# The opening of a two-block transformer kernel: modulation columns and first projection in one program

## What is computed

```python
mod = jax.nn.silu(c) @ w_ada[l] + b_ada[l]          # c: 1 x 1024, w_ada: 1024 x 6144
sh1, sc1, g1, sh2, sc2, g2 = jnp.split(mod[:, None, :], 6, axis=-1)
h = modulate(rmsnorm(x, norm_mix_g[l]), sh1, sc1)    # h * (1 + sc1) + sh1
x = x + g1 * hybrid_mixer(h, w_in[l], ...)           # proj = h @ w_in is its first product
```

## Time and profile before

| | us |
|---|---|
| median of 3 runs | 1884.81 |
| lowest, highest run | 1880.37, 1891.37 |
| profiled execution, its own time | 1885.66 |
| span of the profiled execution | 1883.9 |
| start of the first projection matmul in the span | 48.15 |
| PE busy in the span | 1730.2 |

### The profile page before, as it was taken

One profiled execution on the slowest core, in us unless ns is written; L12 is line 12 of the kernel. 1 busy time (PEld: TensorE's weight loads), 2 busy tenths in 40 slices (PEclk: granted clock), 3 DMA queues, 4 the chain that ended last, 5 costly groups with the idle time before them and its releaser, 6 DMA issues. The chain is left out here.

```text
span 1883.9 us, 20211 instructions
## 1 busy us (share of the span) xinstructions
PE 1730.2 (92%) x8167; PEld 1182.2 (63%) x8167; DVE 805.9 (43%) x1275; ACT 529.4 (28%) x891; POOL 49.2 (3%) x89
## 2 busy tenths in 40 slices
PE   2999989879979999999989999999899989899878
PEld 2887866636668888878768876757334434344346
DVE  4763357632462322255632275234423323233255
ACT  4212246731242222232533242324100000000045
POOL 0000000100000000000000000000200000000000
PEclk8999989999989999999989999999999999999989
DMA  9664120022422222231312011218799999999951
GB/s 354 215 260 139 44 107 28 2 90 90 146 78 90 89 90 90 90 109 59 134 67 101 34 46 45 90 58 347 261 426 426 425 427 427 425 428 426 427 234 45
DMA packets 87655, 351.75 MB, mean 187 GB/s; under 512 B 9910, under 2 KB 39266, under 8 KB 71561
## 3 DMA queue, kind: packets, MB, share of 16 engines
q1 hardware_dynamic: 85002, 346.08, 46.8%
q0 software_dynamic: 2560, 4.37, 0.7%
HBM read 346.03 MB, written 8.43 MB: 188 GB/s over the span
## 5 line engine op out<-in xcount | busy, mean ns | idle before, releaser
L547 DVE TENSOR_TENSOR arena<-ring,arena 128x1024 fp32r<-128x1024 f32 x120 | 146.9, 1225 | 242.9 <-ACT arena L596 223.8
L2651 PE MATMUL ex_h<-ring,u_big_tail 128*64 128x512 f32 x512 | 152.3, 603 | 12.9 <-DMA ring<-in_w 7.8
L552 PE MATMUL up_ps<-h_high,arena 128*128 128x512 f32 x352 | 139.3, 396 | 6.7 <-PEq L178 6.2
L553 PE MATMUL up_ps<-arena 128*128 128x512 f32 x352 | 139.8, 397 | 0.0
L554 PE MATMUL up_ps<-h_high,arena 128*128 128x512 f32 x352 | 139.7, 397 | 0.0
L596 ACT CAST arena<-ring 128x1024 fp32r<-128x1024 f32 x82 | 85.8, 1046 | 167.3 <-PE up_ps L554 88.8
L2651 PE MATMUL ex_h<-s_ab,u_big_tail 128*64 128x512 f32 x272 | 114.3, 596 | 2.3 <-DVE u_big_tail L2622 1.4
L2622 DVE TENSOR_TENSOR u_big_tail<-ex_x,vcol 128x512 f32<-128x512 f32 x32 | 20.6, 687 | 179.7 <-PE ex_x L2615 169.7
L2651 PEld LDWEIGHTS ex_h<-ring,u_big_tail 128*64 128x64 f32 x512 | 47.1, 138 | 76.7 <-issue 75.7
L2917 ACT ACTIVATE u_big_tail<-ex_h 128x512 f32<-128x512 f32 x16 | 9.6, 597 | 292.5 <-PE ex_h L2651 292.5
L552 PEld LDWEIGHTS up_ps<-h_high,arena 128*128 128x128 f32 x352 | 66.5, 189 | 23.4 <-issue 6.6
(11 more groups left out here) (578 smaller groups left out, 3593.8 us busy)
## 6 DMA issues: line engine op xcount, KB each, us to landing
ring<-in_w SPq DMA_DIRECT2D x42, 2048.0 KB, 32.6
s_ab<-in_w SPq DMA_DIRECT2D x32, 2048.0 KB, 31.9
ring<-in_w_in SPq DMA_DIRECT2D x19, 2048.0 KB, 8.0
ring<-in_w_ada SPq DMA_DIRECT2D x24, 1024.0 KB, 6.8
reg_a<-in_w SPq DMA_DIRECT2D x10, 2048.0 KB, 31.9
w1flat<-in_w SPq DMA_DIRECT2D x10, 2048.0 KB
ring<-in_w_ffn_gate SPq DMA_DIRECT2D x11, 1024.0 KB, 5.3
ring<-in_w_ffn_up SPq DMA_DIRECT2D x11, 1024.0 KB, 7.8
```

The lines of the kernel that those rows point to most:

```text
L547: return engine.tensor_tensor(lo, v, hi.bitcast(F32), ALU.subtract)
L552: nc.tensor.matmul(ps, x[0], y[0], start=start, stop=False)
L553: nc.tensor.matmul(ps, x[0], y[1], start=False, stop=False)
L2651: mm = nc.tensor.matmul(ps[half, :], xT[:, k, half], ws[j][:, k, cols], start=(k == 0), stop=(k == k_end - 1))
```

## The change

`stage_modulation` keeps only the name of the row buffer. Its work moves into a class `Opening`, whose methods are called at the head of each engine's list in `stage_project1`; the barrier between the two is gone. In it

- SP loads `c` directly into a column block of `vcol`, 8 neighbouring values for each partition, ahead of `x`; the nine small vectors and `g_ffn_2` (also directly as columns) come between slabs 1 and 2; and 128 columns of `w_in` (`w_first`, 0.5 MB) come ahead of slab 7, as the first unit of the projection.
- DVE adds slabs 0 to 4 only (`ON_DVE = 5`). PE sums `acc` against ones, and slabs 5, 6 and 7 each with their own column of silu(c) as the moving operand, straight from `ring`. The 16 columns are split into two groups with a PSUM bank each, `g` 0 and 1, for feature tiles 0 to 3 and 4 to 7.
- PE's transposes no longer wait for a slab. ACT copies them to a place of their own (`raws`), takes epsilon and 1/D into its root, and loads that table ahead of `x`.
- ACT writes the high part of `h` directly from `raws` with scale and bias (L449 of the new file), and for tiles 1, 3 and 5 (`ON_ACT`) also the full value (L452); DVE makes the full value of the other five (L420) and all low parts. The casts L582 of eight tiles are gone.
- POOL clears `acc2` after the sums are done and after the first unit has been used.

The core of the diff; lines of plumbing are left out:

```diff
+    def sync(self, sp):
+        b, a = self.b, self.b.a
+        sp.dma_start(b.vcol[:, NV + KD:NV + 2 * KD], a["c"].rearrange("a (p k) -> (a p) k", p=P)).then_inc(self.c_in, 16)
+        sp.dma_start(b.x[:], a["x"][0].rearrange("(t p) d -> p t d", p=P)).then_inc(self.x_in, 16)
+        for k in range(KD):
+            if k == 2:
+                for name, n in VROWS:
...
+            if k == KD - 1:
+                sp.dma_start(self.w_first, feature_tiles(a["w_in"][0], 0, P)).then_inc(self.w_in, 16)
+            sp.dma_start(self.piece(k), b.ada1[:, k, :]).then_inc(self.landed[k], 16)
...
+    def tensor(self, pe):
...
+        pe.wait_ge(self.cols_out, 1)
+        for g in range(2):
+            nc.tensor.matmul(psc[g][:, 0:2 * KD], b.ident[:], bias, start=True, stop=False, skip_group_check=True)
+
+        def column_sums(slab, by, g, stop=False):
+            for i in range(2):
+                for k in range(4 * g, 4 * g + 4):
+                    n = i * KD + k
+                    mm = nc.tensor.matmul(psc[g][:, n:n + 1], slab[:, n * P:n * P + P], by, start=False,
+                                          stop=stop and i == 1 and k == 4 * g + 3, skip_group_check=True)
+            return mm
+        pe.wait_ge(self.slabs, ON_DVE)
+        for g in range(2):
+            column_sums(self.acc, b.ones[:, 0:1], g)
+        for k in range(ON_DVE, KD):
+            pe.wait_ge(self.landed[k], 16)
+            for g in range(2):
+                mm = column_sums(self.piece(k), b.sc[:, k:k + 1], g, k == KD - 1)
+                if k == KD - 1:
+                    mm.then_inc(self.summed, 1)
+            if k % 2 and k < KD - 1:
+                mm.then_inc(b.ring_used[k // 2], 1)
...
+            for k in range(4 * g, 4 * g + 4):
+                if k in ON_ACT:
+                    dve.wait_ge(self.made_a, ON_ACT.index(k) + 1)
                 else:
-                    dve.wait_ge(added, k)
...
+                    dve.wait_ge(self.raw, k + 1)
+                    nc.vector.tensor_scalar(b.hT[:, k, :], self.raws[k], b.mulcol[:, k:k + 1], b.modcol[:, k:k + 1],
+                                            ALU.mult, ALU.add).then_inc(self.made, 1)
+                    dve.wait_ge(self.made, k + 1 - sum(j < k for j in ON_ACT))
+                dve.wait_ge(parts.h_hi, k + 1)
+                lower(nc.vector, parts.h[1][:, k, :], b.hT[:, k, :], parts.h[0][:, k, :]).then_inc(parts.h_lo, 1)
...
+        parts.act_w(act, 0)
+        for k in range(KD):
+            act.wait_ge(self.raw, k + 1)
+            act.wait_ge(self.mul, k // 4 + 1)
+            nc.scalar.activation(parts.h[0][:, k, :], self.raws[k], ACT.Identity, scale=b.mulcol[:, k:k + 1],
+                                 bias=b.modcol[:, k:k + 1]).then_inc(parts.h_hi, 1)
+            if k in ON_ACT:
+                nc.scalar.activation(b.hT[:, k, :], self.raws[k], ACT.Identity, scale=b.mulcol[:, k:k + 1],
+                                     bias=b.modcol[:, k:k + 1]).then_inc(self.made_a, 1)
...
         @block.gpsimd
         def _(pool):
+            op.pool(pool)
+            pool.wait_ge(op.summed, 2)
+            pool.wait_ge(parts.used, 1)
             nc.gpsimd.memset(b.acc2, 0.0).then_inc(cleared, 1)
```

More of the change, by code:

```diff
@@ L267 @@
          ("g_ple_2", 8), ("hg_norm_g_2", 4), ("hg_lb_param_2", 8), ("gm_b_sp_2", 8), ("b_ada", 48)]
-BY_ROWS = ["g_ffn_2", "c"]
 VAT = {}
@@ L274 @@
 VAT_ROWS = _n
-NV = _n + 2 * KD
+NV = _n
 def stage_constants(b):
@@ L281, in stage_constants @@
     b.ones = b.sb("ones", [P, P])
-    b.vcol = b.sb("vcol", [P, NV])
+    b.vcol = b.sb("vcol", [P, NV + 2 * KD])
     b.sc = b.sb("silu_c", [P, KD])
@@ L291, in stage_modulation @@
 def stage_modulation(b):
[L301 to L309, removed]
@@ L749, in stage_project1 @@
             units.append((b.c_in[c], b.chunk(b.c_in[c])[:, :, n0:n0 + P], False))
+    units[0] = ("first", b.s_ab[:, 18 * U:20 * U].rearrange("p (k n) -> p k n", k=KD), False)
     gates = [u for c in b.c_merge1[0][0] for u in units_T(b, c)]
@@ L752, in stage_project1, with unit_in @@
     b.early.enter_context(b.parts_area())
-    b.early_parts, b.early0 = Parts(b, "p1", units + gates), len(units)
+    def unit_in(eng, c):
+        if c == "first":
+            eng.wait_ge(op.w_in, 16)
+        else:
+            b.wait_chunk(eng, c)
+    b.early_parts, b.early0 = Parts(b, "p1", units + gates, wait=unit_in), len(units)
     parts = b.early_parts
@@ L756, in stage_project1 @@
         ps = [ps_ctx.enter_context(nc.psum_tensor(f"p1_ps{i}", [P, CH], F32)) for i in range(NB)]
+        op = Opening(b, ps, [ps_ctx.enter_context(nc.psum_tensor(f"op_c{g}", [P, CH], F32)) for g in range(2)])
         block = ps_ctx.enter_context(nc.Block())
@@ L760, in _ @@
         def _(sp):
+            op.sync(sp)
+            sp.wait_ge(op.made, KD - len(ON_ACT))
+            sp.wait_ge(op.made_a, len(ON_ACT))
             sp.dma_start(b.h_dram, b.hTflat[:]).then_inc(b.h_saved, 16)
@@ L780, in _ @@
         def _(pe):
+            op.tensor(pe)
             for i, (c, n0, kind, _) in enumerate(tiles):
@@ L856, in _ @@
         def _(dve):
-            parts.dve_w(dve, 0)
-            parts.dve_h(dve)
+            op.vector(dve, parts)
             for i in range(len(tiles)):
@@ L867, in _ @@
         def _(act):
-            parts.act_w(act, 0)
-            parts.act_h(act)
+            op.scalar(act, parts)
             for i in range(len(tiles)):
```

196 lines of the change are left out of this document (98 added, 98 removed).

## The result

The changed kernel takes 1893.46 us (median of 19 executions, 1888.85 to 1898.81). The kernel before, run beside it on the same chips, takes 1889.41 (19 executions, 1880.37 to 1895.06). The ratio is 1.003, with an interval from 1.0019 to 1.0041: a small loss, within the 0.5% that was called no change. The forecast said 1887 with a range up to 1893, so the time lies just outside, on the slow side.

What follows compares the result with a forecast made beforehand. PE's column sums at the slow clock were taken to bound the opening: first projection matmul at 50.5 instead of 48.15, +2.4 us; 1885.66 + 2.4 = 1888.1, less 0.85 to the median, 1887 us, range 1877 to 1893 (8 in 10).

Steps and rivals of the forecast that it cites:

- What bounds, and the column sums: Opening: PE's 128 sum instructions, mostly at 1.2 GHz, run from 25.0 to 50.5 and set the projection's start; chance 0.72.
- S: Start of the first projection matmul, forecast at 50.5 us instead of 48.15, thus +2.4 us.
- what the transposes leave of the fast level: Start of the column sums: full clock remaining behind PE's transposes, saving 1.5 us, with ends 0 and 2.6.
- the rows between the slabs: Loads: small row vectors and `g_ffn_2` between slabs 1 and 2, taken as 0.6 us, between nothing and 4.3.
- The first unit's tiles of `h`: First projection unit: ACT's eleven pieces take 8.0 us, PE 8.4, so making `h` is hidden with about 1 us.
- Later stages only shifted: Everything behind the opening: the later stages move as a whole by the +2.4 us.
- The median of the kernel before: Starting point: profiled execution 1885.66 us, 0.85 over the median of few runs, which spread from 1880.37 to 1891.37.
- the upper end of 1892: Main forecast's range 1881 to 1892: start 49.4 to 55, slow stretch 1.5 either way, two or three us for the median.
- The loads: Opening: dropping single-element loads, which with rows took 4.3 us, brings slab 4 at 22.0 and slab 7 at 31.3.
- That the sums keep the clock up: Column sums: uninterrupted PE work holds full clock, sets take 3.6 us, 9 us less in all, 1876; chance 0.14.
- The late bias row: First projection units: `b_ada` load waits for POOL's clearing, PE loses 4.6 us, +8.5 with slow sums, 1893; chance 0.12.
- The third, loads that stay where they were: Opening: single-element loads weren't the cost; slab 4 added at 28.4, sums end 3.4 later, 1890; within the forecast's range.

Runs made afterwards that it cites:

- e12: Changed kernel with PE taking projection units 0 and 1 interleaved over the tiles of `h`; 1893.94 us, ratio 1.0029 to the kernel before.
- e1: Changed kernel with all eight slabs added by DVE, so PE sums only the finished accumulator; 1886.26 us, ratio 0.998 to the kernel before.
- e8: Changed kernel run again without an edit, for a second profile; 1894.57 us, ratio 1.0017 to the kernel before.
- e5: e1 plus nine unused float32 matmuls of 512 columns on PE while it waits for DVE; 1886.6 us, ratio 0.9985 to the kernel before.
- e9: Changed kernel with DVE adding seven slabs and PE summing the accumulator and slab 7; 1892.66 us, ratio 1.0037 to the kernel before.
- e10: e5 with DVE's last addition in two halves, one for each group of columns; 1886.08 us, ratio 0.9982 to the kernel before.
- e11: e10 with projection units 0 and 1 interleaved and unit 1's weights made ahead of `h`; 1888.93 us, ratio 1.0009 to the kernel before.
- e7: Kernel before with only `c` and `g_ffn_2` loaded directly as columns; 1886.94 us, ratio 0.9974 to the kernel before.
- e2: Changed kernel with each column sum computed as 32 equal columns, one of them read; 1893.27 us, ratio 1.0018 to the kernel before.
- e3: Changed kernel with an unused 128-column transpose of the identity ahead of each column-sum matmul; 1902.62 us, ratio 1.0076 to the kernel before.
- e4: Changed kernel with POOL clearing `acc2` without waiting for the first unit; 1894.67 us, ratio 1.0025 to the kernel before.

## Why the prediction was off

**What bounds, and the column sums: right.** The forecast put PE on the path with sums at 1.2 GHz, S at 50.5. PE was ready at 25.70 (DVE finished slab 4 at 25.64, forecast 24.7), needed 23.9 us instead of 25.5, and S was 49.61, in the second profile 50.11. The term that was mis-sized is what the transposes leave of the fast level, taken as 1.5 us: one full set ran at 2.4 GHz, which saves 3.2 us, over the 2.6 given as the end. It varies from execution to execution: the first set saved 2.4 us in the second profile, and 0.6 in e12. Two small terms went the other way: the rows between the slabs cost 1.0 us, not 0.6 (slab 1 used on landing at 14.66, slab 2 at 18.13, 3.47 apart where a slab takes 2.49), and `x` came 0.6 later than thought. e1 confirms the step from the other side: without three of the four sets, S is 8.4 us earlier.

**The first unit's tiles of `h`: wrong.** This is the step of the prediction that failed: the overlap of the eight tiles with the first unit was held to be complete, and it was put at nothing. "Hidden with about 1 us" counted ACT's eleven pieces and gave PE the 8.4 us of before, called slow throughout, though the clock was back at 53.9 there. Two things failed. DVE's share, a full value and a low part for a tile one behind the other, sets a pace of 1.18 us a tile at the end. And PE comes back to 2.4 GHz 3.8 us into the unit, after which three matmuls need only 0.69; before, DVE had made all eight low parts by 47.32 + 4.90 = 52.22, ahead of the clock's return at 53.9. The unit took 9.17 and 9.15 us against 8.23 and 6.99 of before. At the 49th matmul the changed kernel is behind by 64.60 - 61.24 = 3.4 us (means of two profiles each): 1.7 from S, 1.7 from the first two units. e12 shows 1.5 us of this as supply of `h`, or by the estimate there 2.0 and 1.3 in the two profiles; the clock came back as late behind S on average as before (4.5 us against 4.4), so no other cause is needed.

**Later stages only shifted: right as far as the executions can tell.** The changed kernel's mean is 5.2 us above that of the 19 executions of before beside it, and e8's 3.8 above that of the 35; 3.4 are accounted for. The interval of the ratio reaches from 3.6 to 7.7 us, and what is above 3.4 isn't located. That a shift at the 49th matmul passes through unchanged holds for e1 to within 1.3 us, but not for e5, e9, e10 and e11, whose rests are 4 to 8 us longer than 1889.7 or 1888.5 (the mean of before beside them) less 61.24 (the 49th in its two profiles).

**The median of the kernel before: the larger part of the miss.** The 2.4 us were added to 1885.66 and brought to the median of three, 1884.81. Nineteen executions have it at 1889.41, so 4.6 us of the miss of 6.5 lie in the starting point, not in the change. 1889.41 + 2.2 would have been 1891.6. Of the 1.9 us left, the first two units are +1.7, the better S -0.7 (1.7 instead of 2.4), and 0.9 isn't located. The working had allowed "two or three us for the median of few runs", though the three themselves spread over 11. And the upper end of 1892 doesn't come out of the terms named for it: 1884.8 + 6.9 for a start at 55 + 1.5 + 2.5 is 1895.7.

**The loads: the outcome near, the reason wrong.** The first slab did come early, but by its place in the queue; e7 shows that the loads of single elements, taken to cost most of 4.3 us, cost S 0.65. Slab 7 was forecast to land at 31.3 and came at 31.98 in e1, where DVE waits for it.

**The rivals.** That the sums keep the clock up is rejected by the changed kernel (20 us of them at 0.50), by e2 and by e3. The Trainium skill ("TensorE: Matmul & The Clock Gate", section "Why this matters for your kernels") asks for a TensorE kept busy without a break; here it was, for 24 us, and the clock fell within them and stayed down. By that rule the change would have gained 9 us. The late bias row is rejected as well, by the changed kernel's own trace: it landed 2.3 us behind the clearing, where 3.7 was the point at which PE would wait. The third, loads that stay where they were, is rejected for this kernel (slab 4 was added by 25.64, not 28.4), though in e7, where the single-element loads alone are changed, it is nearly right.

## What to carry to other kernels

Before moving a sum from one engine to another, compare the price of one step with the interval at which its input arrives, at both levels of TensorE's clock: 2.35 us on VectorE is less than a slab's 2.5, 6.8 on TensorE isn't, and here an overlap that began 10 us earlier didn't pay for it. When preparation is moved beside its consumer, give the first tiles a pace of their own, engine by engine, at the consumer's faster clock. Take the time of the kernel before from enough executions before a change of 0.2% is added to it: three gave 1884.81, nineteen 1889.41.

## What the runs showed of the hardware

- Float32 column sums with 128 x 128 weights cost 0.11 us an instruction at 2.4 GHz and 0.21 at 1.2, the latter with 32 moving columns as with 1 (changed kernel, e2), and 128 of them without a pause did not keep the granted clock up: it fell 3.8 us behind the first, or 0.7 (e12), as it fell in PE's idle waits in e1 and e9 (28.3, 25.9). It fell too with a 128-column transpose ahead of each (e3). Products of 512 columns ahead of them held it (e5: 2.4 GHz until 37.2, where e1 had lost it at 28.3).
- A clearing of 128 x 4096 on POOL stretched a 0.54 us VectorE instruction on 128 x 512 to 3.90 us (e4).
- Starting the projection earlier paid less than its distance: e5 and e10 are at the 49th matmul 1.7 and 2.5 us ahead of e1, and their rest is longer by 2.7 and 1.5. From there to 192 us their waits on PE are those of e1 (2.3 us in all) and only the lengths of the slow spells differ. Whether those spells answer to what came before them, or this is the spread of one profile each, is not settled; the same question stands over the rests of e9 (1834.9), e11 (1833.9) and e7 (1825.0).
